# GpSimd takes the sums of h in the up projection of an encoder's MLP

## The reference, cut to what matters

```
x = layer_norm(ALPHA * x + heads @ w_out)      # 2560 tokens x 1024
h = square(relu(x @ w_ff1))                    # w_ff1: 1024 x 4096
x = layer_norm(ALPHA * x + h @ w_ff2)          # w_ff2: 4096 x 1024
```

## Time and profile before

| | us |
|---|---|
| three runs | 2422.47, 2421.66, 2422.86 |
| median | 2422.47 |
| the profiled execution | 2422.82 |
| its span, first to last instruction | 2421.2 |

### The profile page before, as it was taken

The page is one execution under the profiler, slowest core; times in us unless marked ns, Lnnn a source line. Parts: engine busy times, 40 slices in busy tenths (PEclk is TensorE's granted clock), DMA queues, the critical chain, the costliest instruction groups (busy, mean ns, idle before and its releaser), DMA issues. The chain is left out here.

```text
span 2421.2 us, 34853 instructions
## 1 busy us (share of the span) xinstructions
PE 2362.3 (98%) x12028; PEld 2065.8 (85%) x12028; DVE 1568.6 (65%) x2206; ACT 1101.7 (46%) x1819; POOL 182.9 (8%) x245
## 2 busy tenths in 40 slices
PE   7999999999999899999999999999999999999998
PEld 6888887999888789999999788888888888888887
DVE  8555366765666587786666655556566866774557
ACT  4111146887211155556555544445444444443333
POOL 2000001221223200000000000000000100000002
PEclk9999999999999999999999999999999999999999
DMA  8766766223466666677677755558877797787663
GB/s 302 285 266 228 272 203 223 79 65 90 137 217 217 248 257 259 239 272 279 232 262 262 281 209 199 199 199 306 277 227 216 259 306 226 210 273 264 192 193 120
DMA packets 220608, 547.85 MB, mean 226 GB/s; under 512 B 21704, under 2 KB 90952, under 8 KB 200908
## 3 DMA queue, kind: packets, MB, share of 16 engines
q1 hardware_dynamic: 204416, 488.19, 58.0%
q0 software_dynamic: 16080, 58.20, 7.6%
HBM read 365.95 MB, written 180.36 MB: 226 GB/s over the span
## 5 line engine op out<-in xcount | busy, mean ns | idle before, releaser
L71 PE MATMUL e_bank<-e_hi,e_lo 128*128 128x512 f32 x1120 | 435.8, 389 | 0.1
L73 PE MATMUL e_bank<-e_hi 128*128 128x512 f32 x1120 | 435.7, 389 | 0.0
L72 PE MATMUL e_bank<-e_lo,e_hi 128*128 128x512 f32 x1120 | 435.7, 389 | 0.0
L2353 DVE TENSOR_TENSOR e_lo<-e_raw,e_hi 128x896 fp32r<-128x896 f32 (+1 forms) x168 | 189.9, 1135 | 127.0 <-ACT e_hi L2308 126.7
L2308 ACT CAST e_hi<-e_raw 128x896 fp32r<-128x896 f32 (+1 forms) x168 | 165.2, 983 | 204.0 <-PE e_bank L73 196.8
L71 PEld LDWEIGHTS e_bank<-e_hi,e_lo 128*128 128x128 f32 x1120 | 210.3, 188 | 44.4 <-DVE e_lo L2353 1.0
L73 PEld LDWEIGHTS e_bank<-e_hi 128*128 128x128 f32 x1120 | 210.3, 188 | 43.7
L72 PEld LDWEIGHTS e_bank<-e_lo,e_hi 128*128 128x128 f32 x1120 | 210.3, 188 | 43.6
L71 PE MATMUL u_bank<-u_x_hi,u_wa_lo 128*128 128x384 f32 (+1 forms) x576 | 207.4, 360 | 4.0 <-ACT c_vt_raw L2055 3.6
L71 PE MATMUL u_bank<-u_x_hi,u_wb_lo 128*128 128x384 f32 (+1 forms) x576 | 203.4, 353 | 5.1 <-DVE u_x_first L1883 3.6
L73 PE MATMUL u_bank<-u_x_hi,u_wa_hi 128*128 128x384 f32 (+1 forms) x572 | 205.9, 360 | 0.0
(11 more groups left out here) (332 smaller groups left out, 4888.5 us busy)
## 6 DMA issues: line engine op xcount, KB each, us to landing
u_w_sum<-s_ws SPq DMA_DIRECT2D x33, 1024.0 KB, 4.8
c_vt_raw<-w_ff SPq DMA_DIRECT2D x24, 1024.0 KB, 7.0
c_q_raw<-w_ff SPq DMA_DIRECT2D x24, 1024.0 KB, 7.3
s_h<-c_k_raw SPq DMA_DIRECT2D x32, 768.0 KB, 6.7
e_raw<-s_t SPq DMA_DIRECT2D x96, 256.0 KB, 3.8
e_raw<-s_h SPq DMA_DIRECT2D x112, 192.0 KB, 2.8
ab_place<-w_ff SPq DMA_DIRECT2D x18, 1024.0 KB, 8.2
s_h<-c_k_raw SPq DMA_DIRECT2D x96, 192.0 KB, 2.7
```

The lines of the kernel that those rows point to most:

```text
L71: tensor.matmul(out, w_lo, m_hi, start=first, stop=False, skip_group_check=again)
L72: tensor.matmul(out, w_hi, m_lo, start=False, stop=False, skip_group_check=again)
L73: return tensor.matmul(out, w_hi, m_hi, start=False, stop=last, skip_group_check=again)
L2353: dve.tensor_tensor(part(lo, n), part(raw, n), part(hi, n).bitcast(F32), ALU.subtract).then_inc(split, 1)
```

## The change

`h_sums` moves from VectorE's program to GpSimd's, with the same waits, the same four operations and the two drains. GpSimd now runs over the pairs as the other engines do. The load of one operand becomes a function, `load_x`, with its wait. In groups 0 and 1 the loads whose place is free are asked for in pair NP - 5 ahead of that pair's sums (in group 0 after a wait for the last stored tokens); the others in the last pair, behind that pair's sums. The sums that a pair takes are those of the pair before it. So that pair NP - 5 is written out, `pairs` writes out the last six pairs of each group instead of the last four, on every engine, and the loop is one step (two pairs) shorter.

```diff
--- before.py
+++ after.py
@@ -1771,10 +1771,10 @@
             for g in range(len(UP_GROUPS)):
                 body(g, 0, 0, True, False)
                 body(g, 1, 1, False, False)
-                with eng.Fori(1, NP // 2 - 2) as i:
+                with eng.Fori(1, NP // 2 - 3) as i:
                     for s in range(2):
                         body(g, i * 2 + s, s, False, False)
-                for p in range(NP - 4, NP - 1):
+                for p in range(NP - 6, NP - 1):
                     body(g, p, p % 2, False, False)
                 body(g, NP - 1, 1, False, True)
 
@@ -1864,16 +1864,48 @@
         @block.gpsimd
         def _(pool):
 
-            for g in range(len(UP_GROUPS)):
+            def load_x(g, j):
+                freed = X_FREED[g][j] if g else None
+                if g:
+                    pool.wait_ge(prod_done, (g * NP - 5) * NPROD if freed is None else (g * NP - 1) * NPROD + freed + 1)
                 q = first_pair(g)
-                if g < 2:
-                    pool.wait_ge(mix_st[g], 16 * (NT // 4))
-                for j in range(0 if g else X_FIRST, NPROD):
-                    if g:
-                        freed = X_FREED[g][j]
-                        pool.wait_ge(prod_done, (g * NP - 5) * NPROD if freed is None else (g * NP - 1) * NPROD + freed + 1)
-                    pool.dma_start(x_slot(g, j, False).rearrange("p q k c -> p q (k c)"),
-                                   xb_d[q:first_pair(g + 1), :, j, :].rearrange("q p c -> p q c")).then_inc(x_ld[j], 16)
+                pool.dma_start(x_slot(g, j, False).rearrange("p q k c -> p q (k c)"),
+                               xb_d[q:first_pair(g + 1), :, j, :].rearrange("q p c -> p q c")).then_inc(x_ld[j], 16)
+
+            def h_sums(n, w):
+
+
+                for c in h_done:
+                    pool.wait_ge(h_done[c], n + 1)
+                pool.wait_ge(h_sum_st, 16 * n + 16)
+                pool.tensor_tensor(h_sum[:, 0, 0:w], h[:, 0, 1, 0:w], h[:, 1, 1, 0:w], ALU.add)
+                pool.tensor_tensor(h_sum[:, 2, 0:w], h[:, 0, 0, 0:w], h[:, 0, 1, 0:w], ALU.subtract)
+                pool.drain()
+                pool.tensor_tensor(h_sum[:, 1, 0:w], h_sum[:, 0, 0:w], h[:, 0, 0, 0:w], ALU.subtract)
+                pool.drain()
+                pool.tensor_tensor(h_sum[:, 3, 0:w], h[:, 1, 0, 0:w], h_sum[:, 1, 0:w], ALU.subtract
+                                   ).then_inc(h_summed, 1)
+
+            def body(g, p, s, start, end):
+                n = g * NP + p
+                early = g < LAST and isinstance(p, int) and p == NP - 5
+                if early:
+                    if g == 0:
+                        pool.wait_ge(mix_st[1], 16 * (NT // 4))
+                    for j in range(NPROD):
+                        if X_FREED[g + 1][j] is None:
+                            load_x(g + 1, j)
+                if not start or g:
+                    h_sums(n - 1, UP_GROUPS[g - 1 if start else g][1])
+                if end and g < LAST:
+                    for j in range(NPROD):
+                        if X_FREED[g + 1][j] is not None:
+                            load_x(g + 1, j)
+
+            pool.wait_ge(mix_st[0], 16 * (NT // 4))
+            for j in range(X_FIRST, NPROD):
+                load_x(0, j)
+            pairs(pool, body)
 
         @block.vector
         def _(dve):
@@ -1917,20 +1949,6 @@
                 dve.tensor_tensor(wb_lo[:, 1:3, :], sums[:, 2:4, :], wb_hi[:, 1:3, :].bitcast(F32), ALU.subtract)
                 dve.tensor_tensor(wb_lo[:, 0, :], w_raw[s][:, 2, :], wb_hi[:, 0, :].bitcast(F32), ALU.subtract
                                   ).then_inc(wb_split, 1)
-
-            def h_sums(n, w):
-
-
-                for c in h_done:
-                    dve.wait_ge(h_done[c], n + 1)
-                dve.wait_ge(h_sum_st, 16 * n + 16)
-                dve.tensor_tensor(h_sum[:, 0, 0:w], h[:, 0, 1, 0:w], h[:, 1, 1, 0:w], ALU.add)
-                dve.tensor_tensor(h_sum[:, 2, 0:w], h[:, 0, 0, 0:w], h[:, 0, 1, 0:w], ALU.subtract)
-                dve.drain()
-                dve.tensor_tensor(h_sum[:, 1, 0:w], h_sum[:, 0, 0:w], h[:, 0, 0, 0:w], ALU.subtract)
-                dve.drain()
-                dve.tensor_tensor(h_sum[:, 3, 0:w], h[:, 1, 0, 0:w], h_sum[:, 1, 0:w], ALU.subtract
-                                  ).then_inc(h_summed, 1)
 
             def body(g, p, s, start, end):
                 n, w = g * NP + p, UP_GROUPS[g][1]
@@ -1952,8 +1970,6 @@
                     if g != 1:
                         x_low(g, 4)
                     x_low(g, 5)
-                if not start or g:
-                    h_sums(n - 1, UP_GROUPS[g - 1 if start else g][1])
                 if g == 0 and not start and not end:
                     w_sums(n + 1, 1 - s, isinstance(p, int) and p == 1)
                 if more and not (start and g == 0):
```

## The result

| | before | after |
|---|---|---|
| median of 4 runs, us | 2422.66 (2421.66 to 2423.82) | 2453.07 (2449.26 to 2454.00) |
| span of the profiled execution, us | 2421.2 | 2452.3 |
| mean granted clock | 0.991 | 0.986 |

The ratio is 1.0119, 95% interval 1.0104 to 1.0134: 30.4 us slower, where 14 us were forecast.

The account below looks back on a forecast made before the run. TensorE, busy 98% of the span, was taken to bound the kernel. 2422.8 + 11.8 (ring) + 3 (late loads) - 1 (relief) = 2436.6, against the median 2436.3; forecast 2436.5 us, range 2420 to 2463.

Parts of the forecast that it names:

- The failed step: Groups 0 and 1, early loads ahead of a pair's sums: issued while GpSimd would wait for the square, costing nothing.
- The ring in group 0: Square of h12 to relu of h11 takes 6.2 us, 0.84 over budget, in 14 pairs of group 0: 11.8 us.
- The budget of 5.36 us: Square to relu may take 5.36 us within a 14.56 us pair; each microsecond above lengthens the pair by one.
- the order of the prediction: Group 0: GpSimd's first sum of h goes at 956.46 to 957.43, ahead of VectorE's second low half of the weights.
- The sum by itself: One GpSimd sum taken as two passes over the columns: 0.97 us for 384 columns, 1.24 us for group 2's 512.
- Groups 1 and 2 hidden: Square to relu takes 5.0 us in group 1, under 5.36, and 6.1 in group 2's longer pairs: no cost.
- The late loads: Next group's loads, behind the last pair's first sums, issue about 6 us later: 1.5 us per group start, 3 in all.
- Relief at the starts: Freed VectorE time shortens waits for the last operand's low half at the group starts: 1 us gained, of 0 to 3.6.
- The store of the sums: SP's store of the sums moves some 2 us later with the relu and lands ahead of the next square: no cost.
- two more pairs written out: Two more pairs per group written out instead of looped: 0 us, at most 3.6 us.
- Inside the groups TensorE does not wait: Up projection before the change: TensorE's waits stand only at phase entry and group starts, so the gain's ceiling is 7.2 us.

Follow-up runs that it names:

- the semaphores: The changed kernel with the two drains between GpSimd's sums replaced by waits on a semaphore that the sums count up: 2439.66 us, ratio 1.0062.
- the extra sum: The version with semaphores for the drains, with the third sum taken twice in 15 pairs of group 1: 2450.22 us, ratio 1.0109.
- the version that shares the sums between the engines: Changed kernel with group 0's sums on VectorE, later ones on GpSimd; semaphores for drains, h12 wait last, first late load ahead: 2422.29 us, ratio 0.9995.

## Why the prediction was wrong

- **The failed step** is the sentence on the early loads: "Three early ones (two in group 1) stand before a pair's sums, issued while GpSimd would wait for the square: nothing." The issue is indeed free (1035.94 to 1038.25, the square's release behind it). But the change also moved two drains behind these loads, and the drain waits for their landing: 6.00 and 5.06 us of GpSimd, 5.15 and 3.89 us of TensorE, and 2 to 3 us of half clock each time. Measured: 13.9 us in the trace, 13.4 between the medians of the changed kernel and of the semaphores (15.7 with each against its own batch). The 0.2 us that the prediction gave the drains in its sum for group 1 is near what they took without such loads, twice 0.15 us. The step counted the instructions that are issued and not what stands behind them on that queue. In the kernel before, no drain stood behind these loads in GpSimd's part of this phase.
- **The ring in group 0** (11.8 us): 8.5 us. The budget of 5.36 us was right: four chains over it, by 0.83, 0.15, 0.16 and 0.71 us, lengthened their pairs by about as much. That the loop pairs came out as forecast (15.4; 15.34 to 15.40 measured, chain 6.19 for 6.2) is in part luck: two errors cancel. The turns were shorter than written out, and in the loop the second low half went ahead of the first sum, not behind it. With the order of the prediction the chain was 5.51 us and the pair 14.67; 14 such pairs would have cost some 2 us. The count was wrong too: outside the loop the first sum mostly came first, and pairs 10, 12 and 14 took 14.67, 14.86 and 14.87 us, pair 13 15.23.
- **The sum by itself**, 0.97 us and 1.24 us in group 2: 1.01 us and 1.28 to 1.29. Two passes over the columns was the right reading of the cast in the earlier trace rows. The Trainium skill's "GPSIMD Engine Reference", section "3.1 Elementwise — side-by-side cycle accounting", scaled to 384 columns, would have said 0.84 us, an estimate; the measurement decides. The Trainium skill's rule in "SBUF — State Buffer", section "Who interferes with whom", agrees with 1.53 against 1.01 us on GpSimd and 1.51 against 0.68 us on VectorE.
- **Groups 1 and 2 hidden**: right but for the pair with the drain and pair 14 of group 1 (14.56 us; 18.96 to 19.12 in group 2), and the extra sum shows that the budget of group 1 was real.
- **The late loads** (3 us of 0 to 12): 5.9 us net of the relief. Mis-sized: nearer the middle of its bounds. The place, ScalarE waiting with the P1 copy behind it, was right. Two parts were missing: the first load landed 7.9 us after its issue, with three more right behind it, and 4.6 us where it was asked for alone ahead of the sums (4.7 before); and the half clock behind TensorE's longer waits.
- **Relief at the starts** (1 us): TensorE's two waits for the last operand's low half fell from 3.6 to 2.5 us, in the changed kernel and with only the sums of the first pairs on GpSimd, but they were 3.9 us in the version that shares the sums between the engines. In the times no change can be measured; 1 us is less than their intervals can tell, so this stays open.
- **The store of the sums, two more pairs written out** (0 us each): nothing speaks against either; the kernel with six pairs written out shows the second by itself.
- **"Inside the groups TensorE does not wait"** was not quite so: it waited 0.97 and 0.45 us in group 0 (at 876.98 and 907.36). Nothing hung on it.

With 13.9 us for the drain in place of 0 and the other terms as forecast, the sum would have been 2450.5 us. In it the ring's 3.3 us too many and the 3.9 too few for the starts (late loads less relief) nearly cancel.

## What to carry to other kernels

When arithmetic goes to an engine that also asks for transfers, look at every drain that comes with it: on GpSimd it waits for the transfers that GpSimd asked for, so order two dependent instructions there with a semaphore, or keep the loads on another engine (not tried here). Where GpSimd's instructions and VectorE's hold each other up, who begins first decides the price; put the wait that is met last at the end of the list of waits. And a stop of TensorE can cost more than its length: here 5 us became 7.

## What was not expected of the hardware

- GpSimd's drain held 10.52 and 8.15 us with only a memset of 0.12 us before it, and ended 0.4 us after the last landing of GpSimd's own loads.
- The clock of TensorE stood at 0.50 after an idle time of 5.15 us, which cost some 2 us.
- Two instructions that begin 0.02 us apart in the other order change a pair by 0.65 us, though both wait only for one another's end.
- The last of the three early loads, which landed after 8.7 to 11.0 us in the other runs shown, took 14.1 us once (the early loads behind the sums).
